# Squares of the state space tiles added on GpSimd before the multiplication by ones

## The chip, the cores and the metric

The kernel is one program on one core of a Trainium2 chip. Its engines are TensorE (matrix products, results in PSUM), VectorE, ScalarE and GpSimd (elementwise work), and queues that issue DMAs. The metric is the device time of one launch in microseconds; the median of three runs is given.

## The reference

One inference step of a two-layer encoder trunk in float32, for one prompt of 1024 frames and eight sequences of 16 frames, together nine tiles of 128 frames. The first layer runs an RWKV-7 mixer and a Mamba-2 state space mixer side by side behind one input projection, the second an HGRN2 mixer; each is followed by a gated feed-forward net. The change is in the last lines of the Mamba-2 mixer:

```python
def group_rms_norm(x, w, groups, eps=1e-5):
    x32 = x.astype(jnp.float32).reshape(*shp[:-1], groups, shp[-1] // groups)
    y = x32 * lax.rsqrt(jnp.mean(x32 * x32, axis=-1, keepdims=True) + eps)
    return y.reshape(shp) * w.astype(jnp.float32)

def mamba2_mixer(p, conv_prev, s0, conv_w, conv_b, dt_bias, a_log, d_skip, norm_w, chunk):
    ...
    y, s_new = ssd_chunked(xs, dt, ...)          # 16 heads of 64: W_B = 1024 features
    y = y + d_skip[:, None] * xs
    y = y.reshape(*y.shape[:2], W_B) * jax.nn.silu(z.astype(jnp.float32))
    return group_rms_norm(y, norm_w, G_B), conv_new, s_new        # G_B = 2 groups of 512
```

For every frame the squares of 512 features are summed, once for each of two groups.

## The kernel before

The program is a row of phases. The state space mixer is one of them, `mamba_tiles`. It goes over nine tiles of 128 frames: tiles 0 to 7 are the prompt, tile 8 (`LAST`) holds the eight sequences. The order of work on each engine is written out by hand, in one loop per engine, and the engines meet through semaphores; `wait_ge` waits, `then_inc` signals. An engine does its own instructions strictly in the order written.

The output y of a tile lies with features on the partitions: eight feature tiles of 128 features x 128 frames, four to each group. Its norm goes through these steps:

- `square(t)` on ScalarE writes the squares, 128 x 1024, into `squares(t)`. For the prompt's tiles this is the place in `act` where the output of tile t+1 will stand, for the last tile the buffer `zt`. It signals `sq_done`.
- `square_sum(t)` on TensorE multiplies a matrix of ones with each feature tile of squares and adds four of them in PSUM, for each of the two groups: eight products of 128 x 128 x 128 (L2824). Each float32 product shows as two pairs of weight load and matmul in the trace. The squares are the moving side. It signals `ss_mm`.
- `root(t)` on ScalarE takes logarithm and exponential (L2504, L2507), giving `rs`, 1 over the root of the mean square.
- `finish(t)` on VectorE multiplies y by weights and `rs` into the output (L2589, eight instructions).

In step t of the loops TensorE does, in this order: `inter(t)` (L2712; in the last step L2720, with sequence states), `square_sum(t-1)`, `intra(t)` (L2730, products of `att` and `xd`), then `turn_x(t+1)` (L2739, which needs the load of x), `grams`, `turn_sequence`, `turn_y(t)`, `state(t)` and `segments(t+1)` (L2761). VectorE does `inter(t)` (L2573), `finish(t-1)`, `intra(t)` (L2582, which needs TensorE's L2730), and at the end of the step `gate(t)` (L2632), `to_end(t+1)` (L2638) and `scores(t+1)` (L2644, two instructions, `att` times the masked `CBm`, both in SBUF). `intra(t)` on TensorE needs `att_done` of these scores. ScalarE does half of `spread_decays` (L2480), `root(t-1)`, the other half, the exponentials of the segments (L2493), and last `square(t)` (L2498).

GpSimd has little to do in the phase: three small instructions for a mask, one that clears `C_e`, and, once x of the last tile is loaded, four copies into `C_e` (L2559), which TensorE's L2720 needs.

Of the kernel before, what the change touches and what calls it, by code (L numbers as in the profile page):

```python
# [18 lines left out]
ALU = mybir.AluOpType  # L19
# [9 lines left out]
NT = T // P  # L29
# [2355 lines left out]
def first_mixers_of(nc, g, A, rwkv_out, shift_out, conv_out, ssm_out):  # L2385
    with ExitStack() as outer:
        keep = lambda name, shape: outer.enter_context(nc.sbuf_tensor(name, shape, F32))
        shared = keep("mixer_shared", [P, (4 + NS) * PAIRS * HDA])
        states = shared[:, :].rearrange("p (b j v) -> p b j v", j=PAIRS, v=HDA)
        rw_S, rw_S_samples = states[:, 0:4], states[:, 4:4 + NS]  # L2390
        rwkv_tiles(nc, g, A, rw_S, rw_S_samples)
        S, S_samples = keep("mb_S", [P, 2, WB]), keep("mb_S_samples", [P, NS, WB])
        decays = Decays(nc, outer)
        xbc = keep("mb_xbc", [P, 2, NXBC, P])
        first_x, states_in = nc.alloc_semaphore("mb_first_x"), nc.alloc_semaphore("mb_states_in")

        def early(sp):
            sp.dma_start(xbc[:, 0, :, :], columns_of(g, JX, NAB, 0)).then_inc(first_x, 16)
            for b in range(NS):
                sp.dma_start(S_samples[:, b, :].rearrange("p (j n) -> p j n", n=NBS),  # L2400
                             A["state_ssm"][b, 0].rearrange("(j h) p n -> (h p) j n", h=2)).then_inc(states_in, 16)
        between(nc, g, A, rw_S, rw_S_samples, early, decays, rwkv_out, shift_out, conv_out)
        mamba_tiles(nc, g, A, S, S_samples, decays, shared, xbc, first_x, states_in, ssm_out,
                    first_of(A["w_out_ab"][0], kt=6))
# [7 lines left out]
def mamba_tiles(nc, g, A, S, S_samples, decays, shared, xbc, first_x, states_in, ssm_out, following):  # L2412
# [4 lines left out]
    with Phase(nc, "mamba") as ph:  # L2417
# [11 lines left out]
        squares = lambda t: g.act[:, PAIRS:KACT, (t + 1) * P:(t + 2) * P] if t < NT - 1 else zt[:, :, :]  # L2429
# [1 line left out]
        bank = ph.ps("bank", [P, 8, BANK])  # L2431
        (x_in0, x_in1, z_in, mask_set, RL_done, xT, xd_done, CB_mm, CB_done, B_out, seg_mm, seg_out, att_done, xde_done,
         inter_mm, intra_mm, y1_done, y2_done, st_mm, S_scaled, S_done, yT, skip_done, yz_done, sq_done, ss_mm, var_ln,
         rs_done, out_done, Ce_done, xde_split, seq_scaled, seq_T, seq_in, last_T, last_out) = ph.sems(
            "x_in0 x_in1 z_in mask_set RL_done xT xd_done CB_mm CB_done B_out seg_mm seg_out att_done xde_done "
            "inter_mm intra_mm y1_done y2_done st_mm S_scaled S_done yT skip_done yz_done sq_done ss_mm var_ln "
            "rs_done out_done Ce_done xde_split seq_scaled seq_T seq_in last_T last_out")
        stored = ph.sems("out0 out1 out2")
        x_in = (x_in0, x_in1)
        block = ph.block()  # L2440
        LAST = NT - 1
# [8 lines left out]
        @block.sync  # L2450
        def _(sp):
            for u in range(NT):
                if u >= 2:
                    sp.wait_ge(skip_done, u - 1)
                    sp.wait_ge(inter_mm, u - 1)
                if u:
                    sp.dma_start(xbc[:, u % 2, :, :], columns_of(g, JX, NAB, u)).then_inc(x_in[u % 2], 16)
                    sp.wait_ge(yz_done, u)
                sp.dma_start(zt[:, :, :], columns_of(g, JZ, JX, u)).then_inc(z_in, 16)
            for i in range(SEQS):  # L2460
                sp.wait_ge(last_out, 2 * i + 2)
                dst_ = ssm_out[0][0, 0] if i == 0 else ssm_out[1][i - 1, 0]
                sp.dma_start(dst_.rearrange("(j h) p n -> (h p) j n", h=2),
                             rows[:, row_of(i), :].rearrange("p (j n) -> p j n", n=NBS)).then_inc(stored[row_of(i)], 16)
                if i == NS - 1:
                    sp.wait_ge(st_mm, NTP + NS)
                    load_first(g, sp, following)
            for u in range(3):
                sp.wait_ge(stored[u], 16 * 3)
# [75 lines left out]
        @block.gpsimd  # L2545
        def _(pool):
            tt = nc.gpsimd.tensor_tensor
            pairs = g.blockmask[:, :].rearrange("p (i e) -> p i e", e=2)
            tt(mask_e[:, :], pairs[:, 0, :], pairs[:, 1, :], ALU.add).then_inc(mask_set, 1)
            for i in range(2, 4):  # L2550
                pool.wait_ge(mask_set, i - 1)
                tt(mask_e[:, :], mask_e[:, :], pairs[:, i, :], ALU.add).then_inc(mask_set, 1)
            nc.gpsimd.memset(C_e[:, :, :, :], 0.0).then_inc(mask_set, 1)
            pool.wait_ge(*x_ready(LAST))
            pool.wait_ge(mask_set, 4)
            v = lambda ap: ap.rearrange("p g (i e c) -> p g i e c", e=2, c=BLK)
            for e in range(2):
                for gr in range(2):
                    ins = nc.gpsimd.tensor_copy(v(C_e[:, :, e, :])[:, gr, :, e, :],  # L2559
                                                v(xbc[:, LAST % 2, KB + 2:NXBC, :])[:, gr, :, e, :])  # L2560
            ins.then_inc(Ce_done, 1)

        @block.vector
        def _(dve):
# [136 lines left out]
        def _(pe):  # L2701
# [112 lines left out]
                ins.then_inc(st_mm, 1)  # L2814

            def square_sum(t):
                pe.wait_ge(sq_done, t + 1)
                if t < LAST:
                    pe.wait_ge(seg_out, 4 * (t + 2))
                else:  # L2820
                    pe.wait_ge(y1_done, NT)
                for i in range(2):
                    for j in range(4):
                        ins = mm(bank[:, sums_at(t), i * P:(i + 1) * P], g.ones[:, :], squares(t)[:, 4 * i + j, :],  # L2824
                                 start=(j == 0), stop=(j == 3))
                ins.then_inc(ss_mm, 1)

            for t in range(-1, NT):
                u, mid, front = t + 1, 0 <= t <= LAST, t + 1 <= LAST
                if mid:  # L2830
                    inter(t)
                if 1 <= t:
                    square_sum(t - 1)
                if mid:
                    intra(t)
                if t == LAST:
                    turn_last(0)
                if front:
                    turn_x(u)
                    grams(u)  # L2840
                    if mid:
                        turn_sequence(t, 0)
                if mid:
                    turn_y(t)
                    if t < LAST:
                        state(t)
                if front:
                    if mid:
                        turn_sequence(t, 1)
                    for i in range(4):  # L2850
                        segments(u, i)
            sequence_state(0)
            sequence_state(1)
            square_sum(LAST)
            for b in range(2, NS):
                turn_last(b - 1)
# [675 lines left out]
```

## Time and profile before

| | |
|---|---|
| median of three runs | 3924.93 us (3922.59 to 3927.53) |
| the profiled execution, its span | 3928.0 us |
| TensorE busy | 3679.2 us, 94% |
| VectorE busy | 1981.8 us, 50% |
| ScalarE busy | 698.3 us, 18% |
| GpSimd busy | 943.3 us, 24% |
| mean granted TensorE clock | 0.968 |
| the state space phase | about 967 to 1150 us of the span |

For the profiled execution the record gives the span from its first to its last instruction and nothing around it. PE is TensorE's matmuls, PEld its weight loads, which overlap them; DVE is VectorE, ACT ScalarE, POOL GpSimd, SPq the queue that issues the loads. An instruction's duration contains what it stood still after it was issued; idle time before it is in brackets, with what ended it. Busy shares are means over stages with different limits.

### The profile page before, as it was taken

How to read it: one execution, taken by the hardware profiler on the slowest of the kernel's cores; microseconds unless marked ns; L12 is line 12 of the kernel's file. 1: busy time of each engine (PE TensorE's matmuls, PEld its weight loads, DVE VectorE, ACT ScalarE, POOL GpSimd, SP SyncE). 2: the span in 40 equal slices, each digit the busy share in tenths (PEclk: the TensorE clock that was granted, in tenths of full speed). 3: DMA queues.
4: the chain of work that ended last, by engine and by line, in shares of the span. 5: the costliest groups of instructions: out<-in, count | busy, mean ns of one | idle time of the engine just before them, and what ended most of it. 6: DMA issues, size and time to landing. Idle time of an engine off the chain costs nothing. (4 is left out here: it accounts for less than half of the span.)

```text
span 3928.0 us, 70301 instructions
## 1 busy us (share of the span) xinstructions
PE 3679.2 (94%) x30248; PEld 3477.1 (89%) x30248; DVE 1981.8 (50%) x2684; ACT 698.3 (18%) x1096; POOL 943.3 (24%) x769
## 2 busy tenths in 40 slices
PE   7999978887989999999999999978869999999998
PEld 6999967776769999999999999977759999999998
DVE  5543656663974543433445444346665534344345
ACT  2000125553630100000000232034430100000000
POOL 4222222120012322232232322220012322223221
PEclk9999989997999999999999999989979999999999
DMA  6455431103331111111111233222241111111111
GB/s 218 167 172 173 173 90 30 31 13 80 81 88 41 42 30 51 36 46 41 35 51 33 73 115 104 90 89 83 82 119 37 49 38 43 43 35 46 38 43 70
DMA packets 380196, 286.44 MB, mean 73 GB/s; under 512 B 18020, under 2 KB 361570, under 8 KB 373839
## 3 DMA queue, kind: packets, MB, share of 16 engines
q1 hardware_dynamic: 368640, 238.98, 20.5%
q10 hardware_dynamic: 11214, 44.33, 2.8%
q8 instruction: 169, 2.77, 0.3%
q0 software_dynamic: 128, 0.00, 0.2%
q14 instruction: 45, 0.36, 0.0%
HBM read 223.99 MB, written 59.29 MB: 72 GB/s over the span
## 5 line engine op out<-in xcount | busy, mean ns | idle before, releaser
L641 PE MATMUL ffn_acc<-hH,ffn_wH 128*128 128x384 f32 (+1 forms) x2112 | 716.0, 339 | 13.2 <-DVE hL L502 13.2
L641 PE MATMUL ffn_acc<-hL,ffn_wH 128*128 128x384 f32 (+1 forms) x2112 | 716.0, 339 | 0.0
L641 PE MATMUL ffn_acc<-hH,ffn_wL 128*128 128x384 f32 (+1 forms) x2112 | 492.8, 339 | 0.0
L609 POOL CAST ffn_wH<-raw 128x1024 fp32r<-128x1024 f32 (+2 forms) x164 | 142.0, 866 | 1171.0 <-PE ffn_acc L641 1171.0
L641 PEld LDWEIGHTS ffn_acc<-hH,ffn_wH 128*128 128x128 f32 x2112 | 397.4, 188 | 15.4 <-issue 13.6
L641 PEld LDWEIGHTS ffn_acc<-hL,ffn_wH 128*128 128x128 f32 x2112 | 398.0, 188 | 0.6
L641 PEld LDWEIGHTS ffn_acc<-hH,ffn_wL 128*128 128x128 f32 x2112 | 382.4, 189 | 0.0
L641 PE MATMUL ffn_acc<-ffn_uH,ffn_wH 128*128 128x384 f32 x1056 | 358.6, 340 | 7.6 <-POOL ffn_wL L611 7.6
L641 PE MATMUL ffn_acc<-ffn_uL,ffn_wH 128*128 128x384 f32 x1056 | 357.6, 339 | 0.0
L611 POOL TENSOR_TENSOR ffn_wL<-raw,ffn_wH 128x1024 fp32r<-128x1024 f32 (+2 forms) x164 | 317.6, 1937 | 13.1
L1239 ACT ACTIVATE ffn_gated<-ffn_gated 128x1152 f32<-128x1152 f32 x44 | 51.4, 1168 | 1473.4 <-DVE ffn_gated L542 1473.4
L641 PE MATMUL in_ab_acc<-hH,in_ab_wH 128*128 128x384 f32 (+2 forms) x840 | 289.0, 344 | 6.9 <-DVE hL L502 6.9
L641 PE MATMUL in_ab_acc<-hL,in_ab_wH 128*128 128x384 f32 (+2 forms) x840 | 285.4, 340 | 0.0
L641 PE MATMUL in_c_acc<-hH,in_c_wH 128*128 128x384 f32 (+1 forms) x768 | 260.8, 340 | 6.5 <-DVE hL L502 6.5
L1051 DVE SCALAR_TENSOR_TENSOR xT<-ffn_acc,mod,xT 128x768 f32 (+3 forms) x160 | 112.6, 745 | 302.3 <-PE ffn_acc L641 302.3
L641 PE MATMUL in_c_acc<-hL,in_c_wH 128*128 128x384 f32 (+1 forms) x768 | 260.7, 339 | 0.0
L641 PE MATMUL ffn_acc<-ffn_uH,ffn_wL 128*128 128x384 f32 x1056 | 243.5, 339 | 0.0
L536 DVE TENSOR_TENSOR ffn_up<-ffn_acc,ffn_rstd 128x1152 f32<-128x1152 f32 x44 | 59.7, 1357 | 363.8 <-PE ffn_acc L641 363.8
L641 PEld LDWEIGHTS ffn_acc<-ffn_uH,ffn_wH 128*128 128x128 f32 x1056 | 198.1, 188 | 10.8 <-POOL ffn_wL L611 10.8
L641 PEld LDWEIGHTS ffn_acc<-ffn_uL,ffn_wH 128*128 128x128 f32 x1056 | 198.1, 188 | 0.0
L641 PE MATMUL in_ab_acc<-hH,in_ab_wL 128*128 128x384 f32 (+2 forms) x840 | 196.9, 339 | 0.0
L641 PEld LDWEIGHTS ffn_acc<-ffn_uH,ffn_wL 128*128 128x128 f32 x1056 | 190.4, 188 | 0.0
(587 smaller groups left out, 6643.7 us busy)
## 6 DMA issues: line engine op xcount, KB each, us to landing
in_ab_ada<-in_ada_w SPq DMA_DIRECT2D x40, 1024.0 KB, 5.0
raw<-in_w_gate SPq DMA_DIRECT2D x44, 512.0 KB, 3.8
raw<-in_w_up SPq DMA_DIRECT2D x44, 512.0 KB
pT<-in_ab_out ACTq DMA_DIRECT2D x34, 576.0 KB, 3.3
pT<-in_c_out ACTq DMA_DIRECT2D x32, 576.0 KB, 3.8
raw<-in_w_in_ab SPq DMA_DIRECT2D x34, 512.0 KB, 4.9
raw<-in_w_in_c SPq DMA_DIRECT2D x32, 512.0 KB, 4.1
hgrn_kqg<-pT SPq DMA_DIRECT2D x9, 1536.0 KB
```

The source lines that it names most:

```text
L536: nc.vector.tensor_tensor(out, part, r, ALU.mult)
L609: nc.gpsimd.tensor_copy(wH, raw).then_inc(self.hi_half[u], 1)
L611: nc.gpsimd.tensor_tensor(wL, raw, wH.bitcast(F32), ALU.subtract).then_inc(self.split[u], 1)
L641: ins = self.nc.tensor.matmul(self.acc[0:rows, u, c, 0:n], w[:, u, k, 0:rows], x[:, k, c * CH:c * CH + n], start=(k == 0 and w is self.wH ...
L1051: nc.vector.scalar_tensor_tensor(xs, part, gate[:, ds(n, 1), 0:1].rearrange("p o s -> p (o s)"), xs, ALU.mult, ALU.add)
L1239: nc.scalar.activation(gated[:, :], gated[:, :], ACT.Silu).then_inc(silu_done, 1)
```

## The change

In all tiles but the last, GpSimd adds the squares of a group's four feature tiles before TensorE multiplies them by ones. It does so in place, in two instructions: feature tiles 2 and 3 of both groups onto 0 and 1 (512 elements in each partition), then 1 onto 0 (256 elements). The second waits for the first by a semaphore of its own, `half_added`; the result is signalled by `sq_added`. TensorE's `square_sum` then has one product for each group in place of four, and waits for `sq_added` in place of `sq_done`. The last tile keeps its eight products. GpSimd's program gets seven such pairs ahead of the copies into `C_e` and one behind them.

```diff
+            def add_squares(t):
+                v = squares(t).rearrange("p (g n) c -> p g n c", n=4)
+                pool.wait_ge(sq_done, t + 1)
+                tt(v[:, :, 0:2, :], v[:, :, 0:2, :], v[:, :, 2:4, :], ALU.add).then_inc(half_added, 1)
+                pool.wait_ge(half_added, t + 1)
+                tt(v[:, :, 0, :], v[:, :, 0, :], v[:, :, 1, :], ALU.add).then_inc(sq_added, 1)
+            for t in range(LAST - 1):
+                add_squares(t)
             pool.wait_ge(*x_ready(LAST))
             pool.wait_ge(mask_set, 4)
...
             ins.then_inc(Ce_done, 1)
+            add_squares(LAST - 1)
...
             def square_sum(t):
-                pe.wait_ge(sq_done, t + 1)
                 if t < LAST:
+                    pe.wait_ge(sq_added, t + 1)
                     pe.wait_ge(seg_out, 4 * (t + 2))
+                    parts = 1
                 else:
+                    pe.wait_ge(sq_done, NT)
                     pe.wait_ge(y1_done, NT)
+                    parts = 4
                 for i in range(2):
-                    for j in range(4):
+                    for j in range(parts):
                         ins = mm(bank[:, sums_at(t), i * P:(i + 1) * P], g.ones[:, :], squares(t)[:, 4 * i + j, :],
-                                 start=(j == 0), stop=(j == 3))
+                                 start=(j == 0), stop=(j == parts - 1))
                 ins.then_inc(ss_mm, 1)
```

On TensorE this is the order in step 1, before, from the inter products to the transposes of x:

```order
L2712 MATMUL mamba_bank<-mb_S,mb_xbc 128x512 x2
L2824 MATMUL mamba_bank<-act,ones 128x128 x8
L2730 MATMUL mamba_bank<-mixer_shared,raw 128x64 x16
L2739 MATMUL mamba_bank<-ident,mb_xbc 128x128 x8
L2746 MATMUL mamba_bank<-mb_xbc 128x128 x2
```

and now:

```order
L2722 MATMUL mamba_bank<-mb_S,mb_xbc 128x512 x2
L2837 MATMUL mamba_bank<-act,ones 128x128 x2
L2740 MATMUL mamba_bank<-mixer_shared,raw 128x64 x16
L2749 MATMUL mamba_bank<-ident,mb_xbc 128x128 x8
L2756 MATMUL mamba_bank<-mb_xbc 128x128 x2
```

Nothing has changed its place; the square sum (L2824, now L2837) has two products instead of eight. On GpSimd, around the copies into `C_e` (its clearing at L2553 is ahead of both pieces' first rows), with - for before and + for now, where L2558 is the first addition and L2560 the second:

```order
 L2553 MEMSET mamba_C_e 128x512
-L2559 COPY mamba_C_e<-mb_xbc 128x4x16 x4
+L2558 TENSOR_TENSOR act<-act 128x2x2x128
+L2560 TENSOR_TENSOR act<-act 128x2x128
...
+L2568 COPY mamba_C_e<-mb_xbc 128x4x16 x4
+L2558 TENSOR_TENSOR act<-act 128x2x2x128
+L2560 TENSOR_TENSOR act<-act 128x2x128
```

The copies have moved behind seven pairs of additions; the eighth pair is behind the copies.

## Rows read from the trace of the kernel before

**Rows 1.** The page: its first line, and TensorE's share of the span.

```profile
span 3928.0 us, 70301 instructions
PE 3679.2 (94%) x30248; PEld 3477.1 (89%) x30248; DVE 1981.8 (50%) x2684; ACT 698.3 (18%) x1096; POOL 943.3 (24%) x769
```

**Rows 2.** Stretches: length, busy PE, PEld, DVE, ACT, POOL, granted clock, DMA.

```profile
1073.40:1089.50 16.10, 16.10 (x96) 11.45 (x95) 15.46 (x31) 10.22 (x28) 0.00 (x0) 1.00 0.33 83
```

**Rows 3.** Timeline of one tile: start, duration, engine, line, output<-inputs, count [idle before].

```profile
1073.27 1.89 PE L2712 MATMUL mamba_bank<-mb_S,mb_xbc 128*128 128x512 f32 x4
...
1073.97 1.05 ACT L2498 ACTIVATE act<-sumsq 128x1024 f32<-128x1024 f32 x1
...
1074.48 2.35 DVE L2644 TENSOR_TENSOR raw<-raw,mamba_CBm 128x1024 f32<-128x1024 f32 x2
...
1075.07 1.86 PEld L2824 LDWEIGHTS mamba_bank<-act,ones 128*128 128x128 f32 x16 [0.74 <-ACT act L2498]
...
1076.88 3.65 PEld L2730 LDWEIGHTS mamba_bank<-mixer_shared,raw 128*128 128x128 f32 x32
...
1077.25 0.46 ACT L2504 ACTIVATE mamba_rs<-mamba_bank,eps 128x256 f32<-128x256 f32 x1
...
1078.19 2.19 DVE L2589 SCALAR_TENSOR_TENSOR act<-sumsq,colB,mamba_rs 128x128 f32<-128x128 f32 x8 [0.16 <-ACT mamba_rs L2507]
...
1080.71 1.28 DVE L2582 TENSOR_TENSOR mamba_y_tok<-mamba_y_tok,mamba_bank 128x512 f32<-128x512 f32 x2 [0.33 <-PE mamba_bank L2730]
...
1085.57 3.76 PE L2761 MATMUL mamba_bank<-mixer_shared,after 128*128 128x512 f32 x8
...
1089.85 1.05 ACT L2498 ACTIVATE act<-sumsq 128x1024 f32<-128x1024 f32 x1
```

**Rows 4.** Source line L2498: ns min/median/max, first and last start us.

```profile
L2498 ACT ACTIVATE act<-sumsq x8: 1047/1048/1049, 992.4 to 1105.7; 128x1024 f32<-128x1024 f32 x8
```

**Rows 5.** Waits, 976 to 1105 us: total us, times, longest us.

```profile
PEld mamba_bank L2739 <- DMA mb_xbc<-pT: 1.9, 3, 0.8
```

**Rows 6.** Source lines of two GpSimd forms: ns min/median/max, first and last start us.

```profile
L1669 POOL TENSOR_TENSOR raw<-raw x9: 1256/1263/1272, 566.9 to 862.7; 128x512 f32<-128x512 f32 x9
L602 POOL TENSOR_TENSOR out_c_wL<-raw,out_c_wH x1: 729/729/729, 2930.7 to 2930.7; 128x256 fp32r<-128x256 f32 x1
```

**Rows 7.** Timeline of VectorE and GpSimd, first projection; last, source line L502.

```profile
43.59 0.61 POOL L604 CAST in_ab_wH<-raw 128x512 fp32r<-128x512 f32 x1 [28.45 <-POOLq L95]
...
46.56 2.28 DVE L502 SCALAR_TENSOR_TENSOR hL<-xT,scale,hH 128x1024 fp32r<-128x1024 f32 x1
...
47.71 1.60 POOL L600 CAST in_ab_wH<-raw 128x512 fp32r<-128x512 f32 x1
...
48.77 1.62 DVE L502 SCALAR_TENSOR_TENSOR hL<-xT,scale,hH 128x1024 fp32r<-128x1024 f32 x1
...
49.39 2.14 POOL L602 TENSOR_TENSOR in_ab_wL<-raw,in_ab_wH 128x512 fp32r<-128x512 f32 x1
...
L502 DVE SCALAR_TENSOR_TENSOR hL<-xT,scale,hH x32: 1272/2054/2967, 46.6 to 3059.6; 128x1024 fp32r<-128x1024 f32 x32
```

**Rows 8.** Timeline, the last step of the loop.

```profile
1095.96 0.93 POOL L2559 COPY mamba_C_e<-mb_xbc 128x64 f32<-128x64 f32 x4 [127.41 <-DMA mb_xbc<-pT]
...
1106.26 2.35 DVE L2644 TENSOR_TENSOR raw<-raw,mamba_CBm 128x1024 f32<-128x1024 f32 x2
...
1108.71 1.86 PEld L2824 LDWEIGHTS mamba_bank<-act,ones 128*128 128x128 f32 x16 [0.84 <-issue]
...
1110.49 3.65 PEld L2730 LDWEIGHTS mamba_bank<-mixer_shared,raw 128*128 128x128 f32 x32
```

**Rows 9.** Stretches in the second layer's mixer; groups there; timeline of the last square sum.

```profile
2635.50:2638.90 3.40, 1.04 (x27) 0.93 (x27) 2.93 (x6) 0.00 (x0) 0.00 (x0) 1.00 0.02 5
2638.90:2642.30 3.40, 3.40 (x18) 3.40 (x18) 1.74 (x4) 0.00 (x0) 0.00 (x0) 0.50 0.00 0
...
L3331 PE MATMUL hgrn_bank<-act,raw 128*128 128x128 f32 x16 | 4.2, 354 | 2.4 <-DVE act L3161 2.4
...
1122.61 3.49 PEld L2824 LDWEIGHTS mamba_bank<-mamba_zt,ones 128*128 128x128 f32 x16 [2.75 <-ACT mamba_zt L2498]
```

More of the change, by code:

```diff
@@ L2433, in mamba_tiles @@
          inter_mm, intra_mm, y1_done, y2_done, st_mm, S_scaled, S_done, yT, skip_done, yz_done, sq_done, ss_mm, var_ln,
-         rs_done, out_done, Ce_done, xde_split, seq_scaled, seq_T, seq_in, last_T, last_out) = ph.sems(
+         rs_done, out_done, Ce_done, xde_split, seq_scaled, seq_T, seq_in, last_T, last_out, half_added, sq_added) = ph.sems(
             "x_in0 x_in1 z_in mask_set RL_done xT xd_done CB_mm CB_done B_out seg_mm seg_out att_done xde_done "
             "inter_mm intra_mm y1_done y2_done st_mm S_scaled S_done yT skip_done yz_done sq_done ss_mm var_ln "
-            "rs_done out_done Ce_done xde_split seq_scaled seq_T seq_in last_T last_out")
+            "rs_done out_done Ce_done xde_split seq_scaled seq_T seq_in last_T last_out half_added sq_added")
         stored = ph.sems("out0 out1 out2")
```

## Prediction

> **What bounds the kernel now.** The page first: TensorE is busy for 94% of a span of 3928.0 us [rows 1], but that is a mean over stages with different limits, and the change touches only the state space tiles, nine steps between 967 and 1150 us. So the table of stretches comes next. In a steady tile TensorE counts as busy throughout, VectorE for 15.46 of 16.1 us, ScalarE for 10.2, GpSimd for nothing, at a granted clock of 1.00 [rows 2]. VectorE sets the pace: what delays one of its instructions is paid in full, and what shortens TensorE comes back only where VectorE waits for it.
>
> The timeline of one tile shows where the two meet [rows 3]. ScalarE's squares end at 1073.97 + 1.05 = 1075.02. TensorE begins the square sum at 1075.07 and has loaded its last weights at 1076.93; the intra products (L2730), which follow it, begin at 1076.88. Those need VectorE's scores (L2644, two instructions, 1074.48 to 1076.83). So both things that L2730 waits for are there at the same moment. VectorE then waits twice, a little: 0.16 us for rs ahead of `finish` (L2589) and 0.33 us for L2730 ahead of L2582. From squares to squares this tile takes 1089.85 - 1073.97 = 15.88 us; over the first eight it is 1105.7 - 992.4 = 113.3 us in seven intervals [rows 4], 2.1 more than 7 x 15.88. Three waits of TensorE for x, the longest 0.8, lie in it [rows 5].
>
> **The change part by part.**
>
> *TensorE's saving.* Two of eight products stay. Sixteen weight loads take 1.86 us, 0.116 each, so the four that stay (two a product) take 0.47. In seven tiles this alone is worth nothing: L2730 would still wait for the scores.
>
> *The added work.* Between squares and sum now stand two GpSimd additions. The first has 512 elements a partition and two SBUF operands: the nearest row has 1.26 us, nine times alike. The second has 256: the nearest row has 0.73 [rows 6], and I take 0.72. Between two GpSimd instructions of which one waits for the other lie 0.08 us (47.71 + 1.60 = 49.31, then 49.39) [rows 7]. Alone they need 1.26 + 0.08 + 0.72 = 2.06 us; from the end of the squares to that of the scores it is 1.81.
>
> *They will not run alone.* The scores read two SBUF operands, and the squares end inside the first of them. What happens then is seen in the first projection, where VectorE issues L502, also with two SBUF operands, back to back [rows 7]. One L502 runs from 46.56 to 48.84. A GpSimd cast, issued inside it at 47.71, takes 1.60 us where the same form took 0.61, and ends at 49.31. The next L502, queued since 48.77, takes 1.62 instead of the 1.27 that is the shortest, and ends at 50.39, 1.08 behind the cast. GpSimd's subtraction, issued inside that at 49.39, ends at 51.53, 1.14 behind it. So whoever comes second waits for the whole instruction of the other; with both queued they take turns; and a held instruction saves 0.12 to 0.19 us of its own length.
>
> The Trainium skill states this as a rule ("SBUF — State Buffer", section "Who interferes with whom"): a VectorE instruction with two SBUF inputs and a GpSimd instruction that reads SBUF exclude each other for a whole instruction, in order of issue. By it the sum is the one below; without it, that of the third case. The trace agrees, with the 1.60 us of the cast.
>
> In the tile of [rows 3]: the first score ends at 1074.48 + 1.22 = 1075.70. The first addition ends 1.14 later, 1076.84. The second score, held by it, ends 1.22 - 0.19 later, 1077.87, 1.0 late. The second addition, held by that, ends 0.72 - 0.12 later, 1078.47. TensorE starts the sum 0.05 behind, 1078.52, and L2730 at 1078.99 instead of 1076.88: 2.1 us late. The sum's last product starts 0.35 later and takes 0.28; L2504 of ScalarE follows at 1079.28 instead of 1077.25, so `finish` runs until 1078.19 + 2.03 + 2.19 = 1082.4, and VectorE's L2582 waits for L2730 until 1080.71 + 2.1 = 1082.8. All that follows on the three engines hangs on L2582 and L2730 and moves with them. ScalarE's work behind L2504, the spreading of decays, is needed by L2761, which starts 8 us behind it: hidden.
> If VectorE kept its turn instead, the second addition would end at 1076.83 + 1.14 + 0.08 + 0.72 = 1078.77 and L2730 be 2.4 late. If nothing were held, L2730 would start at 1075.02 + 0.05 + 2.06 + 0.05 + 0.47 = 1077.65, 0.8 late. Seven tiles: **+14.7** (5.6 to 16.8); I take the turns, as [rows 7] show them.
>
> *The eighth sum.* In the last step TensorE has L2720 in front and begins the sum at 1108.71, long after the squares [rows 8]. First score ends 1106.26 + 1.22 = 1107.48, then by the same steps 1108.62, 1109.65, 1110.25; sum from 1110.30, L2730 at 1110.77 instead of 1110.49: **+0.3**. The C_e copies stand ahead of this tile's additions on GpSimd and behind all others; they ended at 1096.9, eight us before anyone needs them: 0.
>
> *A wait that goes.* The waits for x stand right behind L2730. Their loads are issued where they were, counted from the squares, and TensorE comes 2.1 us later than before, more than the longest of them: **-2.1**.
>
> *The clock.* TensorE's inter products end at 1073.27 + 1.89 = 1075.16, and then it has nothing until 1078.52. Elsewhere in this trace a stretch with 1.04 us of TensorE work in 3.40, with one wait of 2.4 us for VectorE in it, is followed by one at a granted clock of 0.50, 1.2 in place of 2.4 GHz [rows 9]. There the work ahead of the gap is thin; here it is dense on both sides, but the gap is longer. At 0.50 this same sum loaded its sixteen weights in 3.49 us, against 1.86. A stretch of 3.4 us at 0.50 so costs 3.4 x (1 - 1.86/3.49) = 1.6 us; part of it falls on the gap itself, so I take 1.2 on L2730 and what follows, all on the path. Bounds for a tile: 0 and 1.6. I take five tiles of seven: **+6.0** (0 to 11.2).
>
> Sum: 14.7 + 0.3 - 2.1 + 6.0 = **+18.9 us**. On the profiled execution that is 3928.0 + 18.9 = 3946.9; its span lies 3.1 above the median of the timed runs, 3924.9, which becomes **3943.8**.
>
> For plain elementwise work the Trainium skill ("GPSIMD Engine Reference", section "4.1 Engine selection") prefers VectorE, with GpSimd about twice as slow on two inputs. The trace agrees: 1.26 us for 512 elements against 0.64 for each L2582. By it the additions would belong on VectorE, which has no time free here, and no term changes.
>
> **The rivals.**
> 1. *The forecast*: held additions, and a clock that falls in most tiles. +14 to +24. Chance 0.52.
> 2. *Held additions, clock at 1.00*: for it speaks that there is one gap a tile, between dense stretches; against it [rows 9]. 14.7 + 0.3 - 2.1 = +12.9, 3937.8. Chance 0.24.
> 3. *The additions run beside the scores*: 0.8 a tile, 5.4 in seven (0.77 each); less 1.8 of the x waits; less 1.1 in the last step, where a sum of 0.47 from 1108.90 lets L2730 start at 1109.4. +2.5, 3927.4. Against it are [rows 7]. Chance 0.10.
> 4. *Not slower*: both additions end before the scores do. From 1.3 us for the pair on, TensorE waits for the scores alone, the seven tiles are as before and the last gains the 1.1: 3923.8. GpSimd would have to be a third faster than [rows 6], and unheld. Chance 0.05.
> 5. *Worse*: VectorE keeps its turn and the clock falls in all seven tiles: 16.8 + 0.3 - 2.1 + 11.2 = +26, 3951. Chance 0.09.
>
> **How the numbers follow.** Two kernels of this length can be told apart from about 0.2%, 7.85 us. Cases 1, 2 and 5 lie above that: slower 0.85. Cases 3 and 4 lie within it, of which 0.02 goes to faster, for shifts in other stages (the three timed runs span 4.9 us): same 0.13, faster 0.02. The range goes from below case 2 to case 5: 3930 to 3951.
>
> **What would show it.** After the change: the first GpSimd addition about 2.2 us long, the second about 1.5; the second L2644 about 2.2 instead of 1.22, the first unchanged; L2730 beginning 3.9 instead of 1.9 us behind the squares' end; `finish` waiting about 2 us for rs; squares to squares 18.0 us in tiles at full clock, 19 where the granted clock falls to 0.50; no wait for x. The forecast is wrong if the second L2644 keeps its 1.22 us and the pair sums to 2.0 (case 3), and wrong in its size if the clock holds 1.00 until 1105 us (case 2).

## The result and the profile after

The changed kernel takes 3972.9 us (median of four runs, 3970.6 to 3975.4) against 3924.7 of the kernel before, a ratio of 1.0124 with a 95% interval of 1.011 to 1.0138: 48 us slower. The forecast was 3943.8 us, 3930 to 3951: the right sign, and a loss less than half as large as the real one. The profiled execution spans 3969.5 us, 41.5 more than that of before. All medians and ratios here and below are over undisturbed runs; one run of e5, 5832 us at a mean clock of 0.58, is left out.

One tile of the changed kernel in the timeline, to be read against [rows 3] (start and length in us, engine, line, operation, operands, count; in brackets the idle time before it and what ended it):

```profile
1013.76 1.89 PE L2722 MATMUL mamba_bank<-mb_S,mb_xbc 128*128 128x512 f32 x4
...
1014.45 1.05 ACT L2498 ACTIVATE act<-sumsq 128x1024 f32<-128x1024 f32 x1
...
1015.01 3.42 DVE L2654 TENSOR_TENSOR raw<-raw,mamba_CBm 128x1024 f32<-128x1024 f32 x2
...
1015.58 1.78 POOL L2558 TENSOR_TENSOR act<-act 128x512 f32<-128x512 f32 x1 [19.18 <-ACT act L2498]
1017.43 1.59 POOL L2560 TENSOR_TENSOR act<-act 128x256 f32<-128x256 f32 x1
...
1019.08 0.71 PE L2837 MATMUL mamba_bank<-act,ones 128*128 128x128 f32 x4 [3.43 <-POOL act L2560]
1019.51 6.65 PEld L2740 LDWEIGHTS mamba_bank<-mixer_shared,raw 128*128 128x128 f32 x32
...
1020.78 2.19 DVE L2599 SCALAR_TENSOR_TENSOR act<-sumsq,colB,mamba_rs 128x128 f32<-128x128 f32 x8 [1.14 <-ACT mamba_rs L2507]
...
1026.15 1.92 PE L2749 MATMUL mamba_bank<-ident,mb_xbc 128*128 128x128 f32 x8
1026.39 1.29 DVE L2592 TENSOR_TENSOR mamba_y_tok<-mamba_y_tok,mamba_bank 128x512 f32<-128x512 f32 x2 [3.42 <-PE mamba_bank L2740]
```

The two scores take 3.42 us in place of 2.35, the additions 1.78 and 1.59 in place of the 1.26 and 0.72 they need alone, and the intra products (L2740, before L2730) begin at 1019.51, 4.01 us behind the end of the squares at 1015.50; it was 1.86. So far this is the forecast. But the 32 weight loads of L2740 then take 6.65 us in place of 3.65, the transposes of x (L2749) 1.92 in place of 1.04, and VectorE waits 3.42 us for L2740 where it waited 0.33.

The stretches show why (start:end and length, busy us and instructions of PE, PEld, DVE, ACT and POOL, then the granted clock, the DMA share and GB/s). First the seven intervals from the first squares to the eighth, then the low part of the tile above and what follows it, in the changed kernel:

```profile
991.88:1149.61 157.73, 133.75 (x581) 101.54 (x583) 115.22 (x204) 70.99 (x183) 24.27 (x18) 0.78 0.24 59
1019.80:1030.10 10.30, 10.30 (x51) 10.30 (x51) 5.18 (x13) 3.23 (x10) 0.00 (x0) 0.50 0.01 2
1030.10:1043.70 13.60, 10.17 (x45) 5.59 (x43) 11.34 (x17) 7.86 (x19) 3.37 (x2) 1.00 0.38 97
```

and the same seven intervals before:

```profile
992.45:1105.74 113.29, 111.85 (x665) 79.75 (x667) 107.00 (x204) 70.20 (x183) 0.93 (x4) 1.00 0.33 82
```

The intervals are 44.4 us longer. The granted clock, 1.00 all through before, has a mean of 0.78; with two levels, 1.00 and 0.50 (2.4 and 1.2 GHz), that is 2 x 0.22 x 157.7 = 69 us at the lower one, ten in the tile shown (the second stretch above, in which TensorE is busy throughout). Of the waits in these intervals the one for x [rows 5] is gone. In the changed kernel TensorE's longest wait and the three longest of VectorE are these (engine, what waits <- what ended the wait: total us, times, longest us):

```profile
PEld mamba_bank L2837 <- POOL act L2560: 29.8, 7, 4.3
DVE mamba_y_tok L2592 <- PE mamba_bank L2740: 21.7, 7, 3.6
DVE act L2599 <- ACT mamba_rs L2507: 9.0, 7, 1.7
DVE sumsq L2635 <- PE mamba_bank L2777: 8.1, 7, 1.7
```

VectorE, which sets the pace, is busy for 8.2 us more than before (115.22 against 107.00, the held scores). The rest of the 44.4 us is idle time: it stands idle for 42.5 us in place of 6.3, and its three waits above are 38.8 of them.

### The profile page after: what moved, and what is told of

It is laid out like the page before. It is cut to its first block and busy times, and to the rows that moved or that the text cites. A ratio compares the mean times of both kernels' runs of the same rounds, so it can differ in the third digit from the quotient of the medians.

```text
span 3969.5 us, 70125 instructions
## 1 busy us (share of the span) xinstructions
PE 3694.6 (93%) x30152; PEld 3494.5 (88%) x30152; DVE 1990.9 (50%) x2684; ACT 698.9 (18%) x1096; POOL 971.0 (24%) x785
```

## The experiments

Theory A: of the loss, some 13 us are the additions and the scores holding each other, as forecast, and the rest is the clock, which falls because TensorE has nothing for 3.4 us in each tile. Theory B: the clock is a bystander, and the time is lost to the holding. Further rivals are named with the runs. Ratios are to the kernel before in the same job, its median there 3925.7 to 3926.2 us.

**The pause filled (e1).** Thirteen unused products stand in TensorE's pause:

```diff
+                    pe.wait_ge(seg_out, 4 * (t + 2))
+                    for n in range(13):
+                        mm(bank[:, sums_at(t), 256:384], g.ones[:, :], g.ident[:, :], start=True, stop=True)
                     pe.wait_ge(sq_added, t + 1)
-                    pe.wait_ge(seg_out, 4 * (t + 2))
```

> The changed kernel with 13 products of ones by the identity (128 columns each, result unused) put on TensorE between the inter products and the wait for the additions, in the seven or eight tiles that have the additions. They should take about 3.0 us, less than the 3.4 us in which TensorE has nothing. Theory A (of the 48 us, 13 are the held additions and some 33 are the granted clock, which falls because of that pause): the clock stays at 1.00, the second score is still held to about 2.3 us, L2740 still begins 4.0 us behind the squares' end, and the time is 3924.7 + 13 = 3938. Theory B (the clock is a bystander, the time is lost to GpSimd and VectorE holding each other): the time stays near 3973.

3936.3 us, ratio 1.0028 (1.0018 to 1.0038): 37 us of the 48 are back, by adding 104 products. One tile of this run in the timeline, and then the stretch of that tile:

```profile
1024.82 1.05 ACT L2498 ACTIVATE act<-sumsq 128x1024 f32<-128x1024 f32 x1
...
1025.34 3.43 DVE L2654 TENSOR_TENSOR raw<-raw,mamba_CBm 128x1024 f32<-128x1024 f32 x2
...
1025.95 1.74 POOL L2558 TENSOR_TENSOR act<-act 128x512 f32<-128x512 f32 x1 [14.60 <-ACT act L2498]
1026.47 2.29 DVE L2654 TENSOR_TENSOR raw<-raw,mamba_CBm 128x1024 f32<-128x1024 f32 x1
...
1027.76 1.59 POOL L2560 TENSOR_TENSOR act<-act 128x256 f32<-128x256 f32 x1
...
1029.84 3.65 PEld L2740 LDWEIGHTS mamba_bank<-mixer_shared,raw 128*128 128x128 f32 x32
```

```profile
1024.82:1042.82 18.00, 17.60 (x109) 13.10 (x109) 16.34 (x30) 10.15 (x28) 3.32 (x2) 1.00 0.30 74
```

The scores are held as before the filling (3.43 us for the two, 3.42 there), L2740 still starts 3.97 us behind the squares, but at a clock of 1.00 it loads its weights in 3.65 us and the tile takes 18.0 us, as forecast for a tile at full clock. The seven intervals are 126.0 us, 12.7 more than before the change. So without the pause the clock stays up, while the holding is unchanged, and theory B is out. The products are not free everywhere: in the last step, where TensorE's pause is only 1.60 us in the changed kernel, they put L2740 5.26 us behind the squares instead of 4.03, so some 1.2 us of what is left of the loss is theirs.

**A pause without contention (e2).** In tiles 0 to 6 GpSimd clears `C_e`, which nobody needs before the last step, in place of adding. The kernel leaves the additions out there, so these sums cover one feature tile of four:

```diff
+                if t < LAST - 1:
+                    pool.wait_ge(mask_set, 4)
+                    for k in range(6):
+                        nc.gpsimd.memset(C_e[:, :, :, :], 0.0).then_inc(half_added, 1)
+                        pool.wait_ge(half_added, 6 * t + k + 1)
+                    pool.sem_inc(sq_added, 1)
+                    return
...
-                pool.wait_ge(half_added, t + 1)
+                pool.wait_ge(half_added, 6 * (LAST - 1) + 1)
```

> In tiles 0 to 6 GpSimd clears an unused buffer six times (about 0.6 us each, 3.6 together, no SBUF operand is read) in place of the two additions, so the sum there covers one feature tile of each group instead of four. TensorE's wait is as long as in the changed kernel, but nothing should hold VectorE. Theory A: the second score takes its 1.22 us, the clock falls to 0.50 in every tile as in the changed kernel, and the time stays near 3972 (within 5 us). Theory B (the cost is in the holding): it falls to about 3924.7 + 7 x 2.1 - 2.1 = 3937 or less.

3975.6 us, 1.0125 (1.0107 to 1.0143). A tile of it in the timeline:

```profile
1017.02 2.35 DVE L2661 TENSOR_TENSOR raw<-raw,mamba_CBm 128x1024 f32<-128x1024 f32 x2
1017.57 3.43 POOL L2561 MEMSET mamba_C_e<- 128x512 f32 x6 [19.47 <-ACT act L2498]
...
1021.11 0.71 PE L2844 MATMUL mamba_bank<-act,ones 128*128 128x128 f32 x4 [3.45 <-POOLq L2563]
```

The scores, with GpSimd busy beside them but reading nothing, take 2.35 us as they did before; TensorE's pause is 3.45 us, and the whole loss is there, with the clock at a mean of 0.73 over the seven intervals of the profiled run, which was the longest of four (3984 us). The pause is enough without any holding.

**Additions behind the scores (e4).** A wait is added ahead of the first addition:

```diff
                 pool.wait_ge(sq_done, t + 1)
+                pool.wait_ge(att_done, t + 2)
```

> The additions wait for the scores as well as for the squares, so neither engine holds the other: both scores 1.22 us, additions 1.26 and 0.72. They then end 2.06 us behind the scores, L2740 begins about 4.5 us behind the squares' end, 0.5 later than in the changed kernel. Theory A: the pause of TensorE is 3.9 us, the clock falls in every tile, and the time is 3973 + 7 x 0.5 = 3976. Theory B (holding is the cost): faster than the changed kernel by 7 us or more.

3983.8 us, 1.0143 (1.0123 to 1.0163). Nobody is held (scores 2.35, additions 1.26 and 0.72), TensorE's pause is 3.99 us, and the kernel is 11 us slower than the changed one in place of the 3 expected. L2741 begins 4.6 to 4.9 us behind the squares (4.73 in the tile shown), where 4.5 had been expected; in seven tiles that is some 4 us against the changed kernel. The mean clock of the seven intervals, 165.5 us, is 0.76, which is 79 us at the lower level in place of 69, some 5 us by the price of 0.46 worked out below. A tile of this run in the timeline:

```profile
1017.62 2.35 DVE L2655 TENSOR_TENSOR raw<-raw,mamba_CBm 128x1024 f32<-128x1024 f32 x2
...
1020.12 1.26 POOL L2559 TENSOR_TENSOR act<-act 128x512 f32<-128x512 f32 x1 [21.17 <-DVE raw L2655]
1021.47 0.72 POOL L2561 TENSOR_TENSOR act<-act 128x256 f32<-128x256 f32 x1
...
1022.24 1.02 PE L2838 MATMUL mamba_bank<-act,ones 128*128 128x128 f32 x4 [3.99 <-POOL act L2561]
```

**One addition (e3, again as e11).** The second addition is left out, and TensorE multiplies and adds two parts for each group:

```diff
-                tt(v[:, :, 0:2, :], v[:, :, 0:2, :], v[:, :, 2:4, :], ALU.add).then_inc(half_added, 1)
-                pool.wait_ge(half_added, t + 1)
-                tt(v[:, :, 0, :], v[:, :, 0, :], v[:, :, 1, :], ALU.add).then_inc(sq_added, 1)
+                tt(v[:, :, 0:2, :], v[:, :, 0:2, :], v[:, :, 2:4, :], ALU.add).then_inc(sq_added, 1)
...
-                    parts = 1
+                    parts = 2
```

> Only the first GpSimd addition (512 elements a partition); TensorE does four products instead of two. TensorE's pause shrinks from 3.4 to about 1.8 us, L2740 begins about 3.0 us behind the squares' end, held by the second score, which is still about 2.3 us long. Theory A: with the shorter pause the clock falls in few tiles or none, 3924.7 + 7 x 1.1 - 2.1 = 3930, and up to 3940 if it falls in two. Theory B (holding alone): the first addition holds the second score just the same, so most of the loss stays, 3960 or more.

3934.7 us, 1.0018 (1.0007 to 1.0029), its ten runs between 3925.5 and 3938.1. In the profiled one the pause is 1.71 us, the clock 1.00, the tile 16.96 us. Theory B is out a second time: the second score is held just as long (3.42 us the pair), and most of the loss is gone. A tile of it:

```profile
1041.23 3.42 DVE L2652 TENSOR_TENSOR raw<-raw,mamba_CBm 128x1024 f32<-128x1024 f32 x2
...
1041.85 1.73 POOL L2558 TENSOR_TENSOR act<-act 128x512 f32<-128x512 f32 x1 [15.23 <-ACT act L2498]
1043.63 1.16 PE L2835 MATMUL mamba_bank<-act,ones 128*128 128x128 f32 x8 [1.71 <-POOL act L2558]
```

> The kernel with one addition once more, beside the one with the pause filled. Theory A: the times fall again on both sides of 3930, and where the profiled run is a slow one, the granted clock is below 1.00 between the first and the eighth squares. Rival: one value within 4 us, clock 1.00.

3933.2 us, 1.0017 (1.0007 to 1.0026), 3926.9 to 3938.3. This time the profiled run was a longer one (3934.2), and one tile of the seven stands out; its stretch, from squares to squares, and that of the tile behind it in this run:

```profile
992.13:1013.96 21.83, 20.14 (x87) 15.42 (x86) 16.38 (x30) 10.14 (x28) 1.73 (x1) 0.77 0.25 62
1013.96:1030.96 17.00, 15.24 (x87) 10.43 (x86) 16.29 (x30) 10.14 (x27) 1.77 (x1) 1.00 0.31 77
```

The clock fell in that one and cost it 4.8 us. So behind a pause of 1.7 us the clock fell in one tile of seven here, and in none of the profiled run of e3.

**One addition, pause filled (e10).** The edit of e3 and, in the place of e1's thirteen products, five:

```diff
+                    pe.wait_ge(seg_out, 4 * (t + 2))
+                    for n in range(5):
+                        mm(bank[:, sums_at(t), 256:384], g.ones[:, :], g.ident[:, :], start=True, stop=True)
                     pe.wait_ge(sq_added, t + 1)
-                    pe.wait_ge(seg_out, 4 * (t + 2))
-                    parts = 1
+                    parts = 2
```

> One addition on GpSimd, and 5 unused products (1.2 us) in TensorE's pause, which leaves 0.5 of its 1.7 us. Theory A (in the kernel with one addition the clock fell in some of the timed runs, whose times spread from 3925.5 to 3938.1, and not in the profiled one): with the pause filled the time is 3924.7 + 5.4, the difference of the profiled intervals, 3930, in every run, within 4 us. Rival (the spread has nothing to do with the pause): the same spread and the same median as without the products, 3935.

3926.7 us, 1.0001 (0.9991 to 1.001): not to be told from the kernel before, 6.5 us less than the one with the pause open. The median is nearer to theory A's 3930 than to its rival's 3935, and below both; the spread, 3917 to 3932, is no narrower, so that part of the expectation failed, and that the spread of e3 and e11 comes from the clock is not shown. Its seven intervals are 118.7 us, 5.4 more than before the change; where these come back is not settled, and they are about the width of the interval.

**Seven products in the pause (e6).** The edit of e1 with fewer products:

```diff
-                    for n in range(13):
+                    for n in range(7):
```

> As the kernel with 13 unused products in TensorE's pause, but with 7, 1.6 us of them, so that some 1.8 us of the pause stay, about as much as with one addition. Theory A (a pause that short does not bring the clock down here): the clock stays at 1.00, tiles of 18.0 us, 3937. Theory C (the loss goes with the length of the pause): half of the 33 us of the clock come back, about 3955.

3961.4 us, 1.0089 (1.0074 to 1.0105). The pause that is left is 1.88 us, and the clock falls in six of the seven intervals. Theory A as I had put it is wrong here: a pause that short does bring the clock down. One tile of the six:

```profile
1035.46 0.71 PE L2839 MATMUL mamba_bank<-act,ones 128*128 128x128 f32 x4 [1.88 <-POOL act L2560]
1036.01 6.28 PE L2740 MATMUL mamba_bank<-mixer_shared,raw 128*128 128x64 f32 x32
```

Theory C, in proportion to the pause, is nearer with 3955, but too low: the seven intervals take 148.8 us, 22.9 more than with the pause filled, of the 31.8 that the full pause cost, and 1.88 us are 55% of the pause. One addition, with 1.7 us, lost far less. The work on both sides of the pause differs too: ahead of it stand seven products here and none there, behind it four loads of the sum here and eight there. Which of these decides I have not separated.

**One tile alone (e5).** The additions in tile 3 only:

```diff
-                pool.wait_ge(half_added, t + 1)
+                pool.wait_ge(half_added, 1)
...
-            for t in range(LAST - 1):
-                add_squares(t)
+            add_squares(3)
...
-            add_squares(LAST - 1)
...
-                    pe.wait_ge(sq_added, t + 1)
+                    pe.wait_ge(sq_added if t == 3 else sq_done, 1 if t == 3 else t + 1)
...
-                    parts = 1
+                    parts = 1 if t == 3 else 4
```

> The additions in tile 3 alone, all other tiles as before. Theory A (each tile with a pause of 3.4 us pays by itself, the clock falls once and comes back within 14 us): one low stretch of 6.8 to 10.2 us in the phase, that interval about 21.3 to 22.9 us instead of 16.7, the next as before; in all +5 to +6 us, 3930. Theory D (the clock, once down, needs a longer dense stretch than these tiles have and stays down or falls again): +10 us or more.

3928.8 us, 1.0005 (0.9995 to 1.0014). The timed difference is 2.5 us and no more than the measurement is uncertain, so the expected 5 to 6 is not shown by the times. The profiled run, 3930.9 us, was one of the longer ones; it tells more, in the stretch of tile 3:

```profile
1039.90:1063.89 23.99, 20.56 (x83) 15.99 (x82) 16.50 (x30) 10.14 (x27) 3.36 (x2) 0.72 0.22 56
```

That tile takes 24.0 us where it took 16.7, at a mean clock of 0.72, and the next takes 15.94, as before. In this run one pause cost its own tile and nothing behind it.

**Work behind the pause (e9).** The thirteen products stand at the head of the intra products, behind their waits:

```diff
+                if 1 <= t < LAST:
+                    for n in range(13):
+                        mm(bank[:, 6, 0:P], g.ones[:, :], g.ident[:, :], start=True, stop=True)
```

> The 13 unused products stand behind TensorE's pause instead of in it, ahead of L2740, in tiles 1 to 7. The pause stays at 3.4 us. Theory A (the pause brings the clock down; work behind it does not prevent that): the clock falls in every tile; the products cost 3.0 us at full and up to 5.7 us at half clock on top of the changed kernel: 3973 + 7 x 3 to 7 x 5.7 = 3994 to 4013. If they shorten the low stretches from 10.2 to 6.8 us, 3.4 us at 0.50 less are worth some 1.6 a tile, 3983 to 4000. Rival: the number of TensorE instructions in a tile alone decides, wherever they stand; then the clock stays at 1.00 as with 13 products in the pause, and the time is 3938 + 7 x 3.0 = 3959.

3971.0 us, 1.0119 (1.0104 to 1.0135): 91 products more than the changed kernel, 3.0 us of them in each tile at full clock, and no slower. Theory A had 3983 or more, its rival 3959. Three stretches of a tile of this run, around the pause, at the low clock and behind it:

```profile
1017.60:1021.00 3.40, 1.36 (x12) 1.36 (x13) 2.60 (x3) 1.43 (x5) 1.91 (x2) 1.00 0.97 236
1021.00:1024.50 3.50, 3.50 (x20) 3.50 (x19) 2.19 (x8) 2.65 (x9) 0.00 (x0) 0.52 0.00 0
1024.50:1028.00 3.50, 3.50 (x33) 3.50 (x33) 0.00 (x0) 0.00 (x0) 0.00 (x0) 1.00 0.02 5
```

The clock falls behind the pause as it did, so the rival that the number of products in a tile decides, wherever they stand, is out. But with the ones-by-identity products following it is back at 1.00 after some 3.4 us, and the 32 loads of L2743 run at full clock. So it is in four of the seven intervals; in the last three the clock stays low for 6.8 us. Over all seven its mean is 0.89 of 161.1 us, 35 us at 0.50 against the 69 of the changed kernel. At 0.46 us each the 34 us less are worth some 16, against 21 us of added products; that leaves 5 more than the changed kernel, and the intervals are 3.4 us longer. So how long the clock stays down depends on what comes behind the pause, and behind ours comes L2740.

**The same in another stage (e8).** The kernel before, without additions, with nine unused products where TensorE waits for VectorE in the second layer's mixer [rows 9]:

```diff
             def outputs(t):
+                if t < LAST:
+                    pe.wait_ge(att_out, 4 * t + 1)
+                    for n in range(9):
+                        mm(bank[:, 6, 0:P], g.ones[:, :], g.ident[:, :], start=True, stop=True)
                 pe.wait_ge(att_done, t + 1)
```

> The kernel before, without any addition on GpSimd, and with 9 unused products (2.1 us) on TensorE in the second layer's mixer, in tiles 0 to 7, where TensorE waits 2.3 us for VectorE ahead of the outputs (L3331) and the granted clock falls to 0.50 behind most of these waits. Theory A carried over: the fall goes, L3331 and L3333 run at full clock, 1.6 us less in some seven tiles: 3924.7 - 11 = 3914. Rival: VectorE or ScalarE set the pace there and hide it, or the thin products ahead bring the clock down all the same: no change within 0.2%.

3916.1 us, 0.9974 (0.9964 to 0.9984): faster than both kernels, with 72 products more whose result nobody reads. Two stretches of this run, at the place of [rows 9]:

```profile
2636.80:2640.20 3.40, 3.23 (x45) 2.99 (x45) 2.96 (x6) 0.00 (x0) 0.00 (x0) 1.00 0.02 5
2640.20:2643.60 3.40, 3.40 (x70) 3.28 (x71) 2.00 (x5) 0.26 (x1) 0.00 (x0) 1.00 0.00 0
```

The two stretches hold the added products and the outputs, and are at 1.00, where the outputs of [rows 9] ran at 0.50. The first products of these outputs, before (L3331) and in this run (L3335), with the shortest, median and longest in ns and the first and last start in us:

```profile
L3331 PE MATMUL hgrn_bank<-act,raw x144: 274/394/581, 2638.2 to 2906.8; 128*128 128x128 f32 x144
L3335 PE MATMUL hgrn_bank<-act,raw x144: 275/275/377, 2639.5 to 2896.1; 128*128 128x128 f32 x144
```

Their median falls from 394 to 275 ns, and from the first to the last of them it takes 256.6 us in place of 268.6: the gain of the timed runs, 10 us, is in this stage. From 2600 to 2880 us the mean clock is 0.96, where it was 0.90.

## Why the forecast was wrong

*What bounds the tile*: right. VectorE sets the pace, and nearly all that the intervals grew by is its held scores and its new waits, for L2740, for `rs` and for L2777.

*TensorE's saving is worth nothing in seven tiles*: right. With the pause filled, four loads stand in the place of sixteen and the intervals still grow by 12.7 us, since L2740, behind the sum, waits for the additions.

*The additions do not run alone*: right in every part. By the steps of the forecast the second score ends 1.0 late, the second addition 0.6 behind it, and L2740 begins 3.97 behind the squares; measured are 1.1 (3.42 us for the pair against 2.35), 0.6 and 4.01. The alternation read from [rows 7] is what happened. The rule of the Trainium skill that the prediction draws on ("SBUF — State Buffer", section "Who interferes with whom") has a VectorE instruction with two SBUF inputs contend with a GpSimd instruction that reads SBUF, and not with one that only writes it. The traces agree on both: 3.42 us for the scores beside the additions, 2.35 beside the clearing of e2.

In two details the list of signs did not follow its own working: the first addition lasts 1.78 us, which is 1076.84 less 1075.07, not "about 2.2", and `finish` waits 1.14 us, since VectorE comes later itself.

*The eighth sum +0.3, the x wait -2.1*: right. L2740 begins 4.03 us behind the squares in the last step, 3.70 before; no wait for x is left. Together with the seven tiles the forecast had +12.6 for the intervals at full clock, and e1 measured +12.7.

*The clock*: this is the term that failed, "five tiles of seven: +6.0 (0 to 11.2)". Measured are 157.7 - 126.0 = 31.8 us in the seven intervals. Where the forecast had 19 us for a tile in which the clock falls, such tiles take 21.3 to 23.9. Its price was right: 1 - 1.86/3.49 = 0.47 us lost for each at 0.50, against 31.8 / 69 = 0.46. The time at 0.50 was wrong: 1.2 / 0.47 = 2.6 us in each of five tiles, 13 in all, against 69. I took the one case of [rows 9], a low stretch of 3.4 us behind a pause, for the length of all of them, and made of the uncertainty of one stretch the bound of the term. There, dense products stood behind the pause. Here the intra products do, and with them the clock came back only after 7 to 14 us; e9, which puts the dense ones first, shows 3.4 again in four tiles and 6.8 in three. That it fell in all seven tiles and not in five is the smaller part.

The trace of before could have warned. The last square sum, from which the price was taken [rows 9], stands in a low stretch of twice that length, in this same phase; and in the stage of [rows 9] three of the low stretches are 6.8 us long too.

```profile
1119.90:1123.30 3.40, 2.06 (x5) 0.69 (x4) 3.30 (x4) 1.06 (x1) 0.00 (x0) 0.51 0.00 0
1123.30:1126.70 3.40, 3.40 (x18) 3.40 (x18) 3.40 (x4) 0.27 (x1) 0.00 (x0) 0.50 0.02 5
```

The last step has no clock term in the forecast either, and there the clock fell as well, to a mean of 0.53 from 1155.90 to 1162.70 us of the changed kernel.

The fifth case of the forecast, the worst, was short for the same reason, and with it the upper end of the range. Of the 48 us of the timed runs, 11 are left with the pause filled (e1) and 37 go with the clock.

## What to carry to other kernels

Taking products from an engine that is not the bound gained nothing here, and a wait put in their place can cost more than its length: price a pause of TensorE by its own length and by the time at half clock behind it, and read that time from a place where the same kind of work follows. In a trace, look at the granted clock behind the pauses that recur, short ones too (here it fell behind 1.9 us); where it falls, unused products in the pause can be worth more than they cost (3916 against 3926 us in e8). Before work goes to GpSimd, see whether VectorE's instructions beside it read two SBUF operands, since the two then take turns by whole instructions.

## What was not expected of the hardware

The clock fell with TensorE idle for 1.7 to 1.9 us in tiles that were otherwise dense: in the profiled runs in six tiles of seven in e6 (1.88 us), in one in e11 and in none in e3 (1.7 us). Behind a pause of 3.4 us it stayed at 0.50 for 7 to 14 us, in the tile shown above for 10 in which TensorE had no gap. With 26 matmuls of ones by identity put first it stayed there for 3.4 us in four tiles and 6.8 in three. How the length of the pause and the work on its two sides share in this is open: e9 varies only what comes behind the pause, but e1 and e6 change, with the 0.4 and 1.9 us that are left of it, also the number of products ahead.
